# MLA stage of a two-block transformer kernel: projection blocks of later groups copied by ScalarE, rotation from memory in parts, rotary blocks first

## The reference, cut to what matters

```python
ckr = hn @ w_dkv                      # 256 latent columns and 64 rotary columns
c_kv = rmsnorm(ckr[..., :256], kv_norm)
k_rope = apply_rope(ckr[..., 256:], cos, sin)      # one for all heads
k_nope, v = c_kv @ w_uk, c_kv @ w_uv               # 16 heads of 128 each
c_q = rmsnorm(xn @ w_dq, q_norm)
q = c_q @ w_uq                                     # 16 heads of 128 + 64 rotary columns
q_rope = apply_rope(q[..., 128:], cos, sin)
# per head and block of 128 queries: softmax((qn k_nope + qr k_rope) * scale) @ v, causal
# apply_rope: [x1*cos - x2*sin, x2*cos + x1*sin] on halves of 32
```

## Time and profile before

| | |
|---|---|
| median of 3 runs | 2726.32 us (2720.48 to 2729.05) |
| profiled execution | 2719.7 us, span 2717.9 us |
| units before the loop, loop of items | about 734 to 763 us, 768 to 1000 us of the span |
| PE busy over the span | 95% |
| DVE, ACT, POOL busy | 55%, 24%, 42% |

### The profile page before, as it was taken

One profiled execution on the slowest core, in us unless ns is written; L12 is line 12 of the kernel. 1 busy time (PEld: TensorE's weight loads), 2 busy tenths in 40 slices (PEclk: granted clock), 3 DMA queues, 4 the chain that ended last, 5 costly groups with the idle time before them and its releaser, 6 DMA issues.

```text
span 2717.9 us, 31048 instructions
## 1 busy us (share of the span) xinstructions
PE 2571.4 (95%) x11716; PEld 2044.5 (75%) x11716; DVE 1495.3 (55%) x2046; ACT 663.1 (24%) x1299; POOL 1134.9 (42%) x764
## 2 busy tenths in 40 slices
PE   7999899999988889999999999999989998899998
PEld 6888688888766668888887777777766667688886
DVE  4754565464756634554657584444445777555511
ACT  2003521021323331200213213333322441222200
POOL 4333355555521115555554443333322224455554
PEclk9999899999989989999999999999999999899999
DMA  6334355655522116565564474554464435465655
GB/s 201 124 113 136 112 190 193 194 189 198 186 70 70 62 49 199 186 198 189 191 213 157 154 226 156 161 159 155 139 207 130 146 113 178 141 200 188 197 188 170
DMA packets 149049, 436.61 MB, mean 161 GB/s; under 512 B 14065, under 2 KB 18353, under 8 KB 148913
## 3 DMA queue, kind: packets, MB, share of 16 engines
q1 hardware_dynamic: 64224, 200.29, 24.8%
q0 software_dynamic: 67584, 201.35, 21.2%
q10 hardware_dynamic: 17104, 33.14, 3.6%
HBM read 417.90 MB, written 16.83 MB: 160 GB/s over the span
## 4 chain that ended last, share of the span: by engine, by line
issue 35%; PE 33%; POOL 24%; DVE 4%; DMA 2%; ACT 2%; DVEq 1%; ACTq 0%; POOLq 0%; SPq 0%
POOL w_lo L470 19%; PE bank L522 9%; PE bank L525 8%; PE bank L524 8%; POOL w_hi L452 5%; PE bank L727 2%; DMA projections<-spill_out 1%; PE bank L1154 1%; PE bank L1163 1%; DMA residual<-x_in 1%; PE bank L801 1%; PE bank L804 0%; PE bank L803 0%; PE bank L1121 0%; DVE next_gained L2359 0%
## 5 line engine op out<-in xcount | busy, mean ns | idle before, releaser
L470 POOL TENSOR_TENSOR w_lo<-w_raw,w_hi 128x1024 fp32r<-128x1024 f32 x376 | 902.3, 2400 | 15.5 <-DMA w_hi<-stream 7.0
L452 POOL DMA_DIRECT2D w_hi<-stream x376 | 226.4, 602 | 1549.9 <-PE bank L522 1378.1
L522 PE MATMUL bank<-x_hi,w_hi 128*128 128x512 f32 x1464 | 587.8, 402 | 28.8 <-POOL w_lo L470 15.3
L524 PE MATMUL bank<-x_lo,w_hi 128*128 128x512 f32 x1464 | 573.6, 392 | 0.0
L525 PE MATMUL bank<-x_hi,w_lo 128*128 128x512 f32 x1464 | 573.5, 392 | 0.0
L522 PEld LDWEIGHTS bank<-x_hi,w_hi 128*128 128x128 f32 x1464 | 276.7, 189 | 113.8 <-issue 40.4
L525 PEld LDWEIGHTS bank<-x_hi,w_lo 128*128 128x128 f32 x1464 | 276.7, 189 | 58.7
L524 PEld LDWEIGHTS bank<-x_lo,w_hi 128*128 128x128 f32 x1464 | 277.2, 189 | 55.5 <-issue 2.2
L2075 DVE TENSOR_TENSOR relu_sq<-relu 128x512 f32<-128x512 f32 x64 | 178.6, 2791 | 95.1 <-ACT relu L1456 95.1
L525 PE MATMUL bank<-hidden_hi,w_lo 128*128 128x512 f32 x512 | 199.3, 389 | 0.0
L522 PE MATMUL bank<-hidden_hi,w_hi 128*128 128x512 f32 x512 | 199.3, 389 | 0.0
(11 more groups left out here) (445 smaller groups left out, 4520.0 us busy)
## 6 DMA issues: line engine op xcount, KB each, us to landing
w_hi<-stream POOLq DMA_DIRECT2D x376, 512.0 KB, 4.7
w_raw<-stream SPq DMA_DIRECT2D x376, 512.0 KB, 3.6
projections<-spill_out ACTq DMA_DIRECT2D x56, 256.0 KB, 2.1
ssm_x<-projections ACTq DMA_DIRECT2D x4, 1024.0 KB, 7.0
gate_tiles<-projections ACTq DMA_DIRECT2D x16, 256.0 KB, 3.0
ssm_z<-projections ACTq DMA_DIRECT2D x16, 256.0 KB, 2.6
residual<-x_in SPq DMA_DIRECT2D x4, 512.0 KB, 12.1
toeplitz_hi<-toeplitz_rows_hi POOLq DMA_DIRECT2D x4, 512.0 KB, 6.2
```

The costliest lines, as they stand in the source:

```text
L452: e.dma_start(in_slot(whi, t % SLOTS, o), in_stream(o)).then_inc(hi_ready[t % SLOTS], 16)
L470: e.tensor_tensor(wlo[:, s, :], raw[:, s, :], whi[:, s, :].bitcast(F32), ALU.subtract).then_inc(lo_ready, 1)
L522: mm = e.matmul(out, wh, rh, start=first, stop=False)
L524: e.matmul(out, wh, rl, start=False, stop=False)
```

## The change

ACT now reads the bank of every k, v, q and r block of groups 1 to 3, and also of group 0's two r blocks; an r block is only copied, into one of two new buffers `rope_raw` (`rraw`). DVE rotates it there, in place, from memory: four exchanged multiplications into `rope_sum`, then the multiplication by the cosine, then the addition. For groups 1 to 3 these six instructions and `rope_low` are spread over items: three exchanged pieces at item 8 (first pair) and item 10 (second pair), the fourth with the other two at items 9 and 11, `rope_low` at 11 and 13. ACT's `rope_high` goes to items 10 and 12. The next group's blocks are computed in another order, and the stream's tiles with them: r, k, q, v instead of k, q, r, v, and the last q block goes to item 0 of its own group. The key's rotary part is rotated in the same way, and because `rope_sum` lies in memory that the d units still read, this comes after `unit(1)` instead of before `unit(0)`. Waits of scores and output products are counted by unit.

```diff
-MLA_ORDER += [... (0, 3, 1, 2)] + whole_tiles(FIRST["mla"] + 4, 12)
+MLA_ORDER += [(FIRST["mla"] + 4 * g + t, None) for g in range(1, 4) for t in (2, 0, 1, 3)]
+        rraw = [at(f"rope_raw{x}", kb, [P, S]) for x, kb in enumerate((138, 124))]
-        rt0, rt = at("rope_tmp0", 168, [P, S]), at("rope_tmp", 124, [P, S])
-        GROUP_STEPS = {3: ["v0"], 4: ["v1", "v2"], 5: ["v3"], 7: ["k0"], 8: ["k1", "k2"], 9: ["k3", "q0"], 11: ["q1"],
-                       12: ["q2", "q3"], 13: ["r0"], 15: ["r1"]}
+        GROUP_STEPS = {3: ["v0"], 4: ["v1", "v2"], 5: ["v3"], 7: ["r0"], 8: ["r1", "k0"], 9: ["k1"], 11: ["k2"],
+                       12: ["k3", "q0"], 13: ["q1"], 15: ["q2"], 0: ["q3"]}
-            return (kind in ("k", "v") and g > 0) or kind in ("dq", "ga", "gs", "ql", "ys")
+            return (kind in ("k", "v", "q") and 0 < g and u < UNIT_B0) or kind in ("r", "dq", "ga", "gs", "ql", "ys")
...
 ACT, unit(u):
+                    elif kind == "q":
+                        e.activation(gq[g % 2][:, j, :], bank[6 + u % 2][:, :], ACT.Copy).then_inc(un_act, 1)
+                    elif kind == "r":
+                        e.activation(rraw[j][:, :], bank[6 + u % 2][:, :], ACT.Copy).then_inc(un_act, 1)
+                        e.drain().then_inc(rope_raw, 1)
...
 ACT, loop of items:
+                    if n % 16 in (10, 12) and n < 48:
+                        rope_high(2 * (n // 16 + 1) + n % 16 // 12)
...
 DVE:
+                def exchanged(x, first, n):
+                    if first == 0:
+                        e.drain()
+                    for q in range(first, first + n):
+                        a, b = slice(32 * q, 32 * q + 32), slice(32 * (q ^ 1), 32 * (q ^ 1) + 32)
+                        tt(rsum[a], x[b], rp[b, 1, :], ALU.mult)
+                def rotated(x):
+                    exchanged(x, 3, 1)
+                    e.drain()
+                    tt(x, x, rp[:, 0, :], ALU.mult)
+                    e.drain()
+                    return tt(x, x, rsum[:, :], ALU.add)
+                def rope_step(n):
+                    s, g = n % 16, n // 16 + 1
+                    if s in (8, 10):
+                        pair = 2 * g + (s - 8) // 2
+                        e.wait_ge(rope_raw, pair + 1)
+                        exchanged(rraw[pair % 2], 0, 3)
+                    elif s in (9, 11):
+                        rotated(rraw[(s - 9) // 2][:, :]).then_inc(rope_full, 1)
+                    if s in (11, 13):
+                        rope_low(2 * g + (s - 11) // 2)
...
-                rotated(krr[:, 1, :], rt0[:, :], krr[:, 0, :])
-                e.drain()
-                tt(krr[:, 1, :], rt0[:, :], krr[:, 1, :], ALU.add)
                 unit(0)
                 latent(0, ckv, "kv_norm", rstd_c, ckh, ckl)
                 unit(1)
-                e.drain().then_inc(rope_full, 1)
+                exchanged(krr[:, 0, :], 0, 3)
+                rotated(krr[:, 0, :]).then_inc(rope_full, 1)
...
-                for u in range(6, 16):
+                for u in range(6, 14):
                     unit(u)
-                    if u >= 14:
-                        rope_low(u - 14)
+                for pair in range(2):
+                    e.wait_ge(rope_raw, pair + 1)
+                    exchanged(rraw[pair], 0, 3)
+                    rotated(rraw[pair][:, :]).then_inc(rope_full, 1)
+                for pair in range(2):
+                    rope_low(pair)
```

More of the change, by code:

```diff
@@ L962, in scores @@
                         e.wait_ge(rope_done, 2 + n // 8 + 1)
-                    if g and n % 16 == 0:
-                        e.wait_ge(un_act, 4 * (2 * g - 1))
+                    if g and i == 0:
+                        e.wait_ge(un_act, freed_before(max(MLA_UNIT_AT["k", g, j], MLA_UNIT_AT["q", g, j]) + 1)[0])
                     if n >= 3:
@@ L979, in out_product @@
                         if hh:
[L980 removed]
+                            e.wait_ge(un_act, freed_before(MLA_UNIT_AT["v", hh // 4, 3] + 1)[0])
                         else:
@@ L1497, in rope_high @@
                     e.wait_ge(rope_full, 1 + pair + 1)
-                    e.activation(rqh[rope_slot(pair)][:, :], rsum[:, :], ACT.Copy).then_inc(rope_hi, 1)
+                    e.activation(rqh[rope_slot(pair)][:, :], rraw[pair % 2][:, :], ACT.Copy).then_inc(rope_hi, 1)
                 next_act(T_MLA, xh2, gains("mla_norm", 8))
@@ L1505, in mla @@
                 for x in range(2):
-                    e.activation(krh[x][:, :], krr[:, 1, :], ACT.Copy, scale=own_half[:, x:x + 1]).then_inc(rope_hi, 1)
+                    e.activation(krh[x][:, :], krr[:, 0, :], ACT.Copy, scale=own_half[:, x:x + 1]).then_inc(rope_hi, 1)
+                for pair in range(2):
+                    unit(14 + pair)
                 for pair in range(2):
@@ L2174, in mla @@
                     e.wait_ge(rope_hi, x + 1)
-                    stt(krl[x][:, :], krr[:, 1, :], own_half[:, x:x + 1], krh[x][:, :].bitcast(F32), ALU.mult,
+                    stt(krl[x][:, :], krr[:, 0, :], own_half[:, x:x + 1], krh[x][:, :].bitcast(F32), ALU.mult,
                         ALU.subtract).then_inc(rope_done, 1)
-                for u in range(6, 16):
+                for u in range(6, 14):
                     unit(u)
-                    if u >= 14:
-                        rope_low(u - 14)
-                low_next = None
+                for pair in range(2):
+                    e.wait_ge(rope_raw, pair + 1)
+                    exchanged(rraw[pair], 0, 3)
+                    rotated(rraw[pair][:, :]).then_inc(rope_full, 1)
+                for pair in range(2):
+                    rope_low(pair)
                 for n in range(MLA_ITEMS + 2):
@@ L2195, in mla @@
                         ts(mpr[:, m % 3, 0:w], mpr[:, m % 3, 0:w], mri[:, m:m + 1], None, ALU.mult).then_inc(at_p, 1)
-                    if low_next is not None:
-                        rope_low(low_next)
-                        low_next = None
-                    for u in STEP_UNITS[n]:
-                        if not by_act(u):
-                            unit(u)
-                            if UNITS[u][0] == "r":
-                                low_next = 2 * UNITS[u][1] + UNITS[u][2]
+                    if n < 48:
+                        rope_step(n)
                     if n >= 6 and (n - 6) % 4 == 0:
```

27 lines of the change are left out of this document (8 added, 19 removed).

## The result

The changed kernel takes 2711.65 us in the median of 5 runs (2706.62 to 2715.72), the kernel before, run beside it, 2727.23 us. The ratio is 0.9939, with a 95% interval of 0.9927 to 0.9952: 15.6 us faster, where 3.7 were forecast (2722.6 us). The time lies in the range of 2710 to 2735, only 1.7 us above its low end, and outside the 2718 to 2728 of the likeliest case; the sign is right, the size is four times too small. The profiled execution took 2706.62 us, its span is 2704.7.

A forecast was written before the change was run, and what follows sets the result against it. PE, busy 95% of the span, was taken as the bound, so only its idle time and clock count. Seams -10.2 us and the part before the loop +6.5 gave -3.7 from 2726.3: 2722.6 us, range 2710 to 2735.

The forecast's parts named there:

- the likeliest case: Whole kernel: 10.2 us gained at three seams, 6.5 lost before the loop, 3.7 us faster; chance 0.45.
- The seam's waits: End of each group: PE waits of 0.53, 0.53 and 3.98 us go, new ones total 2.45; 2.6 us gained per seam.
- the new one at item 29: After each seam: w_lo finds DVE in its scaled probabilities, and PE waits 1.8 us anew.
- The 0.65 at item 27: After each seam: DVE's scaled probabilities come 0.65 us after PE needs them, a new wait.
- The third piece at item 24: DVE's third exchanged piece starts 0.66 us before w_lo, so it is just in time and not held.
- the first rival: Item 24: w_lo holds the third piece, a seam gains only 0.7 us, the sum is +4.4, 2730.7 us; chance 0.22.
- The clock: At each seam: one 1.6 us drop to low clock fewer, half a drop (0.8 us) back for the new wait.
- Before the loop: Ahead of the group loop: the key's rotation and group 0's r blocks by way of memory cost 6.5 us together.
- The key's rotation: Behind unit 1: held by w_lo, it delays unit 2's copy and brings a clock drop; +5.5 us.
- The rotary blocks: Group 0's two r blocks, copied by ACT and rotated from memory, start the loop later: +1.0 us, from +0.5 to +2.5.
- The front is cheap: Before the loop: w_lo waits for the key's rotation, costing 1.7 and 0.5 us; sum -8.0 to -10.4, 2717 us; chance 0.28.
- The third rival: At the seam: a 4 us wait remains as items 10 and 11 crowd, no clock gain, 2730 to 2737 us; chance 0.05.

The follow-up runs named there:

- starts: The changed kernel with blocks placed so no tile begins in a head's fourth item, and rotation steps one item later: 2714.66 us, ratio 0.9963 to the kernel before.
- pad8: The changed kernel with eight multiplications, whose product nothing reads, added on DVE at items 15, 31 and 47: 2724.59 us, ratio 0.9996 to the kernel before.
- front_old: The changed kernel with the key's rotation ahead of unit 0 and group 0's r blocks rotated straight from the bank: 2709.55 us, ratio 0.9941.
- k_early: The changed kernel with the key's rotation ahead of unit 0 again, its exchanged pieces in their own buffer: 2707.6 us, ratio 0.9936 to the kernel before.
- starts2: The changed kernel with no tile begun in a head's fourth item and rotation at items 10, 12, 14 and 15: 2696.78 us, ratio 0.9896.
- starts2_k: starts2 with only the key's rotation taken ahead of unit 0: 2696.22 us, ratio 0.9890 to the kernel before.
- starts2_front: starts2 with the key's rotation ahead of unit 0 and group 0's r blocks rotated straight from the bank: 2690.82 us, ratio 0.9863.
- pad6: The changed kernel with six multiplications, whose product nothing reads, added on DVE at items 15, 31 and 47: 2718.73 us, ratio 0.9975 to the kernel before.

## Why the prediction was right, and where it was mis-sized

**The seam's waits: right, 9.7 for 7.8 us.** The three waits of 0.53, 0.53 and 3.98 are gone at each seam, and the new one at item 29 is 1.64 for the 1.8 forecast. The 0.65 at item 27 did not come. In the replay PE was to reach it 12.8 us after item 24's transposes; in after it takes 13.3 us in group 0 at full clock and 14.8 in group 1, and DVE's scaled probabilities are ready just then, as the row at 868.90 shows. The replay, with durations of single rows added up, ran PE a little too fast. By these waits a seam gives 5.04 - 1.64 = 3.4 us for the 2.6 forecast, by the balance of idle time 3.2.

**The third piece at item 24: right.** Neither 855.17 2.07 x3 in group 1 nor the three pieces in group 0 were held:

```profile
798.94 2.07 DVE L2141 TENSOR_TENSOR rope_sum<-rope_raw,rope_table 32x512 f32<-32x512 f32 x3
800.31 0.57 POOL L453 DMA_DIRECT2D w_hi<-stream  x1 [2.76 <-PE bank L523]
800.90 2.40 POOL L471 TENSOR_TENSOR w_lo<-w_raw,w_hi 128x1024 fp32r<-128x1024 f32 x1
```

Here the third starts at about 800.32, 0.58 us ahead of `w_lo`, and runs plain. In group 1 the margin was wider, since PE's low clock moved `w_lo` to 858.65. So the first rival is out, by little. The Trainium skill, page "SBUF — State Buffer", section "SBUF: two separate sides", lets whichever instruction starts first have the ports. By these rows that holds only from a lead of about half a microsecond over the recorded start of `w_lo`: L2164 in starts led by 0.26 and took 3.20.

**The clock: the term that was mis-sized, 9.7 us for 2.4.** The forecast put a drop at 1.6 us, counted one less per seam, and set half a drop against it for the new wait. Three things were off. First, the drop at the seam: the 0.50 of the earlier trace rows is that of a stretch cut at 3.5 us, but the low level goes on to 832.8, and PE works at it for 15.8 us over the three seams, as the rows with pad8 above show. At 0.52 us for each us that is 8.2 us, 2.7 a seam for 1.6. Second, of the shorter falls, 3.4 us each, before had three behind the fourth row maximum (items 8, 40 and 52) and after has two (items 24 and 40): 1.8 us more, in no term of the forecast. front_old, which puts the old front back, has the one at item 8 again, so this part comes from the change before the loop and not from the seams. Together 10.0, measured 9.7; the 0.52 is read from the same busy times, so the sum shows where the clock was lost and is no second proof of its price. Third, the new waits of 1.64 brought no fall, where half a drop each, 2.4 us in all, was charged, as the stretch right behind the one at 874.68 shows (second row), set against the one behind 854.07:

```profile
854.20:858.00 3.80, 3.80 (x12) 3.08 (x13) 2.77 (x7) 1.44 (x4) 0.00 (x0) 0.55 0.18 64
874.70:878.20 3.50, 3.50 (x17) 2.81 (x18) 1.58 (x6) 1.65 (x4) 0.00 (x0) 1.00 0.16 59
```

A lone wait put back at the seam reproduces only part of this: pad8 brought back all the idle time, and 1.9 of the 9.7 us of the clock. Why the old seams held PE at the low level for twice as long stays open.

**Before the loop: right in place and sign, 5.35 for 6.5.** The key's rotation is 3.4 for 5.5: the copy of unit 2 started 0.3 us earlier than forecast, and the expected fall of the clock behind the wait (1.6) did not come. That a wait of 3.98 us brought one at the seam did not mean that one of 3.15 would here. The rotary blocks are 2.0 for 1.0. On DVE the replay holds to 0.1 us up to the end of both `rope_low`: it had this end at 774.1, and 778.48 less the 1.0 at the anchor and the 3.4 of the key is 774.1. What was too small was "some more on PE": the first scores wait for this end (10.03 us), need 1.58 us to the first row maximum, and run into 10.2 us of low clock, where the kernel before had two stretches of 3.4.

**The rivals.** "The front is cheap" described the right size of the total, -8.0 to -10.4, for the wrong reason: `w_lo` did not wait for the key's rotation, the pieces were held as forecast. The real sum, -14.05, was in none of the cases, since all of them took the clock's price from one drop of 1.6 us. That the range still held the time is luck: its low end was reached by way of a cheap start that did not come. A gain of over 0.3% had a chance of 0.32, against 0.55 for no change. The third rival, a wait of 4 us left at the seam, is out: behind the fourth row maximum no wait over 1.8 us is left.

**From the profiles to the medians.** The profiled executions differ by 13.1 us, the medians by 15.6; the sum by the stage windows is 14.05. Behind this stage the profiled executions of all kernels took from 1719.5 us (starts) to 1728.6 (k_early) for the same work, so no more can be read from that.

## What to carry to other kernels

Price a wait on PE together with the clock behind it, and read that price from the busy time of the same instructions over the whole stretch, not from one short window; here the clock gave 9.7 us and the waits 9.7. Where two engines exclude each other, list what the first has queued at every moment at which the second will start, and move either the start or the queued work: moving the tile starts alone lost 4.5 us, moving them with the rotation gained 14.3. Work that had idle time to lie in (the key's rotation) should stay there when the rest is rearranged.

## What the hardware showed that was not expected

- PE's clock falls are not a function of the wait before them. Waits of 1.76 us were followed by one in two cases of six in the kernel after, the waits of 1.64 there in none of three, the one of 3.15 before the loop by none, and of the three of 3.15 in starts two by none and one by 6.8 us at the low level, which began inside it. Three waits of 3.98 were followed by 3.4 us at the low level in pad8 and had 6.8 us around and behind them in the kernel before. Adding waits at one place (pad8) removed falls at another.
- The edge at which `w_lo` holds DVE is sharp in these traces. `rope_low` started 0.53 or 0.54 us ahead of `w_lo`'s recorded start in all nine cases of starts2, starts2_k and starts2_front, and took 0.68 or 0.69 us each time. The gain of the second latent, started 0.47 or 0.48 us ahead in all kernels but pad6 and starts, took 3.42 us each time. It is another kind of instruction (scalar_tensor_tensor), but the kind is not what decides: an addition of two tiles in memory, like `rope_low` a tensor_tensor of 128x512, started 0.48 and 0.47 us ahead in after (at 692.47 and 703.35, in the MLP before this stage) and took 3.43 both times. A read of a bank is not held: `out_low` started 0.45 us ahead in after, at 992.33, and took a plain 0.69. POOL's DMA issue is recorded in the 0.6 us ahead of `w_lo`; whether it has a part in this was not tried. starts2 thus rests on a margin of some 0.05 us at item 13, where a held `rope_low` cost 3.15 us of PE's time in starts.
